# Norm sums through 64 columns, LoRA products beside the residual updates, and attention scores inside the query products

## The reference

```
h = h + 0.5 * rms_norm(swiglu(rms_norm(h, g[0]), w_in, w_out), g[1])   # pre norm, post norm
u = rms_norm(h, g[2])
# mixer: x_prev is x shifted by a token
xr, xw, xk, xv, xa, xg = [x + (x_prev - x) * mu[i] for i in range(6)]
r = xr @ w_rkv[0];  k = xk @ w_rkv[1];  v = xv @ w_rkv[2]
w = -softplus(-(w0 + tanh(xw @ w1) @ w2)) - 0.5
a = sigmoid(a0 + (xa @ a1) @ a2);  g = sigmoid(xg @ g1) @ g2
# attention: blocks of 128 queries against 256 keys, 16 query heads, 4 key heads
q = xq @ w_q + b_q
p = softmax(concat([mask(q k^T / 8), sink]))[..., :-1];  o = (p v) @ w_o + b_o
# last block
mod = c @ w_ada + b_ada
```

## Time and profile before

| | us |
|---|---|
| median of 3 runs | 2849.88 (2849.01 to 2850.76) |
| the profiled execution | 2848.1 |
| its span | 2846.2 |
| PE busy | 2700.0 (95% of the span) |
| DVE busy | 1094.9 (38%) |
| ACT busy | 627.9 (22%) |
| POOL busy | 1783.7 (63%) |
| mean granted TensorE clock | 0.966 of full |

### The profile page before, as it was taken

How to read it: one execution, slowest core, us unless ns; L and a number is a source line. 1 busy time by engine, 2 the same in 40 slices (tenths; PEclk the granted TensorE clock), 3 DMA queues, 4 the chain that set the end, 5 groups by cost and what they waited for, 6 DMA issues and landing times.

```text
span 2846.2 us, 47915 instructions
## 1 busy us (share of the span) xinstructions
PE 2700.0 (95%) x17928; PEld 2199.1 (77%) x17928; DVE 1094.9 (38%) x1624; ACT 627.9 (22%) x1203; POOL 1783.7 (63%) x1827
## 2 busy tenths in 40 slices
PE   8999988988987999999999999899999999999998
PEld 7888877767775788888888888678888888777677
DVE  3333043774554533310533303655333224123344
ACT  2111033433532211101211102343111011344211
POOL 6777768673321577776677766665777756645565
PEclk9999989989998999999999999999999989999998
DMA  4333313220000233333233332332333323322212
GB/s 138 95 95 96 96 45 88 75 57 3 4 3 12 74 89 96 95 96 94 75 96 96 96 96 78 115 133 70 97 96 96 95 72 92 90 62 67 76 42 81
DMA packets 116791, 225.94 MB, mean 79 GB/s; under 512 B 13088, under 2 KB 13856, under 8 KB 115616
## 3 DMA queue, kind: packets, MB, share of 16 engines
q1 hardware_dynamic: 114624, 209.46, 26.1%
q10 hardware_dynamic: 2016, 14.22, 1.4%
HBM read 221.53 MB, written 2.10 MB: 79 GB/s over the span
## 4 chain that ended last, share of the span: by engine, by line
PE 70%; DVE 7%; ACT 3%; issue 3%; POOL 3%; DMA 0%; DVEq 0%; POOLq 0%; ACTq 0%; SPq 0%
PE bank L222 17%; PE bank L224 17%; PE bank L223 17%; PE bank L320 1%; PE bank L1290 1%; POOL turn_a L1978 1%; DVE h L692 1%; PE bank L1305 1%; PE bank L353 1%; PE bank L2224 1%; PE bank L1240 1%; PE bank L240 1%; DVE acc L316 1%; PE bank L2215 1%; PE bank L2406 1%
## 5 line engine op out<-in xcount | busy, mean ns | idle before, releaser
L209 POOL TENSOR_TENSOR w_lo<-w_raw,w_hi 128x512 fp32r<-128x512 f32 x778 | 1045.5, 1344 | 755.5 <-PE bank L224 593.1
L222 PE MATMUL bank<-x_hi,w_hi 128*128 128x512 f32 x1904 | 751.5, 395 | 4.3 <-POOL w_lo L209 2.2
L224 PE MATMUL bank<-x_hi,w_lo 128*128 128x512 f32 x1904 | 747.8, 393 | 0.0
L223 PE MATMUL bank<-x_lo,w_hi 128*128 128x512 f32 x1904 | 742.8, 390 | 0.0
L214 POOL TENSOR_SCALAR w_hi<-w_raw 128x512 fp32r<-128x512 f32 x778 | 569.9, 733 | 4.8 <-DMA w_raw<-weights 4.8
L222 PEld LDWEIGHTS bank<-x_hi,w_hi 128*128 128x128 f32 x1904 | 358.2, 188 | 83.6 <-POOL w_lo L209 4.2
L224 PEld LDWEIGHTS bank<-x_hi,w_lo 128*128 128x128 f32 x1904 | 357.9, 188 | 80.2
L223 PEld LDWEIGHTS bank<-x_lo,w_hi 128*128 128x128 f32 x1904 | 358.1, 188 | 79.2 <-issue 0.2
L659 DVE TENSOR_TENSOR f<-bank,rstd 128x512 f32<-128x512 f32 x88 | 56.7, 686 | 595.5 <-PE bank L224 587.7
L222 PE MATMUL bank<-mid_hi,w_hi 128*128 128x512 f32 x704 | 276.4, 393 | 0.8 <-POOL w_lo L209 0.8
L224 PE MATMUL bank<-mid_hi,w_lo 128*128 128x512 f32 x704 | 276.3, 393 | 0.0
(11 more groups left out here) (426 smaller groups left out, 3584.3 us busy)
## 6 DMA issues: line engine op xcount, KB each, us to landing
w_raw<-weights SPq DMA_DIRECT2D x778, 256.0 KB, 2.6
ada_w<-ada_in ACTq DMA_DIRECT2D x8, 1536.0 KB, 6.7
h<-xT SPq DMA_DIRECT2D x4, 512.0 KB, 7.0
out<-f SPq DMA_DIRECT2D x8, 256.0 KB, 2.2
mask_b<-mask_b_in ACTq DMA_DIRECT2D x1, 640.0 KB, 5.2
spread<-spread_in SPq DMA_DIRECT2D x1, 512.0 KB, 7.5
window<-window_in ACTq DMA_DIRECT2D x1, 512.0 KB, 4.0
masks<-masks_in SPq DMA_DIRECT2D x1, 320.0 KB, 7.0
```

The source lines that it names most:

```text
L209: pool.tensor_tensor(w_lo[:, (n - 1) % RW, :], w_raw[:, (n - 1) % RS, :], w_hi[:, (n - 1) % RW, :].bitcast(F32), ALU.subtract).then_inc(w_ ...
L222: pe.matmul(outs[m], w_hi[:, s, c], hi, start=first, stop=False)
L223: pe.matmul(outs[m], w_hi[:, s, c], lo, start=False, stop=False)
L224: done = pe.matmul(outs[m], w_lo[:, s, c], hi, start=False, stop=last)
```

## The change

It has four parts.

**The mixer's head.** The updates of the first FFN move into `rwkv_vector`. ACT makes `u_hi` and DVE `u_lo` from gain times `h`, without the norm's factor, tile by tile as the updates go; PE runs the LoRA products beside them, the unshifted and the shifted half into separate banks. The factor `rstd` is applied by six DVE operations (`lora_in`) between the first x tiles. Even squares are added on DVE, odd ones on PE. POOL's six small folds become one multiplication of 128x512 with broadcast factors, and `r_gather` is made after them.

The core of the diff, its parts in the order of the text:

```
 # sums
-                done = pe.matmul(out[:, t:t + 1], src[:, t * P:(t + 1) * P], ones[:, 0:1], start=first and t == 0, ...
+                done = pe.matmul(out[:, t * 64:(t + 1) * 64], src[:, t * P:(t + 1) * P], ones[:, 0:64], start=first and t == 0, ...
+        def by_block(sums):
+            return sums[:, 0:64 * TT].rearrange("p (t c) -> p c t", c=64)[:, 0, :]
 # post norm
             unread(1)
+            norm_sums(pe, s.post, bank[s.post_at][0])
             for k in s.post.summed:
                 sum_square(pe, s.post, k, bank[s.post_at][0])
-            norm_sums(pe, s.post, bank[s.post_at][0])
         def output_scalar(act, s):
+            act.preload_act_table_set("sqrt_and_others")
...
-                if m == 3:
+                if m == 1:
                     norm_root(act, s.post, bank[s.post_at][0], D)
 # mixer, vector engine
+            for k in each:
+                update_h(dve, f0, k)
+                if k + 1 < KT:
+                    update_f(dve, f0, k + 1)
+                dve.wait_ge(*ra("u_hi", k))
+                dve.scalar_tensor_tensor(out=u_lo[:, k, 1:T + 1], in0=h[:, k, :], scalar=vcol(s.gain_in, k), in1=u_hi[:, k, 1:T + 1].bitcast(F32),
+                                         op0=ALU.mult, op1=ALU.subtract).then_inc(*rv.tell("u_lo", k))
+                add_square(dve, s.pre, k)
...
+            u_tile(0)
             dve.wait_ge(*rg("omu", 1))
             mixing(0)
+            dve.wait_ge(rstd_ready, s.rs + 1)
             for q in each:
+                if q + 1 < KT:
+                    u_tile(q + 1)
                 tile(q)
+                if 1 <= q < 7:
+                    lora_in(q - 1)
 # mixer, POOL
-                    for j, (i, a, b) in enumerate(((1, 0, 64), (4, 64, 128), (5, 128, 256)) * 2):
...
-                        pool.tensor_scalar(raw[:, c], raw[:, c], factor, None, ALU.mult).then_inc(*rg.tell("fold", k, j))
+                    columns = raw.rearrange("p (g c) -> p g c", c=64)
+                    factors_ = segments[:, k, :].unsqueeze(2).to_broadcast([P, 8, 64])
+                    pool.tensor_tensor(columns, columns, factors_, ALU.mult).then_inc(*rg.tell("fold", k))
 # attention, PE
+            for k in range(2, KT):
+                unit_products(pe, outs, x_hi[:, k, :], x_lo[:, k, :], k == 0, k == KT - 1, s.n_q + KT + k)
+                if k in (2, 4, 6):
+                    scores((2, 4, 6).index(k))
...
+                if i == STEPS:
+                    pe.wait_ge(*ad("mask", STEPS - 1))
+                for b, k in output[i - STEPS:i - STEPS + 1] if STEPS <= i < STEPS + 4 else output[4:] if i == STEPS + 4 else ():
 # attention, vector engine
-                if i in (3, 7, 11, 15):
-                    ada((3, 7, 11, 15).index(i) + 1)
+                if i < 2:
+                    ada(1, 2 * i)
+                    ada(1, 2 * i + 1)
+                elif i % 2 == 0 and 4 <= i <= 18:
+                    ada(2 + (i - 4) // 8, (i - 4) // 2 % 4)
```

More of the change, by code:

```diff
@@ L294, in square_used, with square_at @@
             eng.wait_ge(sq_summed if on_pe else sq_used, n + 1)
+        def square_at(nm, j):
+            return sq_last[:] if nm.late and j == nm.tiles - 1 else sq[:, (nm.sq0 + j) % 2, :]
         def square(act, nm, j, src, **bias):
[L297 to L300, removed]
+            g = nm.sq0 + j
+            if g >= 2 and not (nm.late and j == nm.tiles - 1):
+                square_used(act, g - 2)
+            act.activation(square_at(nm, j), src, ACT.Square, **bias).then_inc(sq_ready, 1)
         def add_square(dve, nm, j):
@@ L319, in sums_of @@
             for t in range(TT):
-                done = pe.matmul(out[:, t:t + 1], src[:, t * P:(t + 1) * P], ones[:, 0:1], start=first and t == 0, stop=last and t == TT - 1,
+                done = pe.matmul(out[:, t * 64:(t + 1) * 64], src[:, t * P:(t + 1) * P], ones[:, 0:64], start=first and t == 0, stop=last and t == TT - 1,
                                  skip_group_check=True)
@@ L340, in norm_root @@
                 act.wait_ge(sums_ready, nm.n + 1)
-            else:
+            if nm.late or not nm.added:
                 square_used(act, nm.sq0 + nm.tiles - 1)
-            act.activation(root[:], sums[:, 0:TT], ACT.Sqrt, bias=eps[:, 0:1], scale=1.0 / width).then_inc(root_ready, 1)
+            act.activation(root[:], by_block(sums), ACT.Sqrt, bias=eps[:, 0:1], scale=1.0 / width).then_inc(root_ready, 1)
         def norm_inverse(dve, nm):
@@ L803, in program @@
         PREP = "cum cm fl kk k2 b K B A0 A".split()
-        rv = Steps("rwkv_dve", ["zero", "reset", "reset0", "gn_eps"] + [("block", n) for n in range(3)] + [("u_lo", k) for k in each] + ["wa_lo", "tg_lo"] +
+        rv = Steps("rwkv_dve", ["zero", "zero_lo"] + [("u_lo", k) for k in each] + ["reset", "reset0", "gn_eps"] + [("block", n) for n in range(3)] +
+                   [(n, j) for j in range(2) for n in ("now", "back", "in")] + ["wa_lo", "tg_lo"] +
                    [(n, 0) for n in PREP[:3]] + ["max", "rec"] + [(n, 0) for n in PREP[3:]] + [(n, k) for k in (1, 2) for n in PREP] + [("R", k) for k in range(3)] + [(n, k) for k in range(3, KT) for n in PREP + ["R"]])
@@ L1460, in flat @@
             return t.rearrange("p a t -> p (a t)")
[L1462 removed]
+        SEGMENTS = (1, 4, 5, 5) * 2
+        rg = Steps("rwkv_pool", [("omu", 0), ("omu", 1)] + [("segment", j) for j in range(8)] + [("fold", k) for k in each] + [("gather", k) for k in each])
         def lora_pool(pool, s):
@@ L1791, in swa_tensor @@
             norm_beside(pe, s, outs, s.n_q + KT, KT - 1)
-            for k in range(2, KT):
-                unit_products(pe, outs, x_hi[:, k, :], x_lo[:, k, :], k == 0, k == KT - 1, s.n_q + KT + k)
             def scores(a):
@@ L1838, in values @@
                 done.then_inc(*ap.tell("value", a))
+            for k in range(2, KT):
+                unit_products(pe, outs, x_hi[:, k, :], x_lo[:, k, :], k == 0, k == KT - 1, s.n_q + KT + k)
+                if k in (2, 4, 6):
+                    scores((2, 4, 6).index(k))
+            output = [(b, k) for b in two for k in each]
             for i in ITERATIONS:
                 for a in step_at(i, 0):
-                    scores(a)
+                    if i >= 3:
+                        scores(a)
                 for a in step_at(i, 3):
@@ L1872, in swa_scalar, with biased @@
             act.activation(rstd[:], bank[s.pre_at][1][:], ACT.Copy).then_inc(rstd_ready, 1)
+            def biased(k):
+                act.wait_ge(*qv("q", k))
+                act.activation(q_t[:, k, :], q_t[:, k, :], ACT.Identity, bias=vcol("b_q", k)).then_inc(*qa.tell("bias", k))
+            for k in range(4):
+                biased(k)
+            NEXT_ADA = (1, 3, 11, 19)
             def next_ada(k):
-                act.wait_ge(*av("ada", k - 1))
-                act.dma_start(ada_w[:], ada_in[k]).then_inc(ada_loaded, 16)
+                act.wait_ge(*av("ada", k - 2, 3))
+                act.dma_start(ada_w[k % 2][:], ada_in[k]).then_inc(ada_loaded[k % 2], 16)
             for i in ITERATIONS:
```

192 lines of the change are left out of this document (107 added, 85 removed).

## The result

The changed kernel takes 2805.02 us in the median of 4 runs (2803.22 to 2807.75), against 2849.45 for the kernel before in the same comparison: a ratio of 0.9846, 95% interval 0.9829 to 0.9863. That is 44 us less where 39 were forecast; the time lies 6 us under the predicted 2811, inside the range. The profiled execution has a span of 2802.2 us against 2846.2, so the two traces show 44.0 of it.

The account below looks back on a forecast made before the run. TensorE, busy 2700.0 of 2846.2 us, was taken as the bound, leaving only stretches with gaps or low clock. Gains of 8.4, 12.4 and 18.1 sum to 38.9, from 2848.1 to 2809.2, as a median 2811 us; range 2802 to 2820.

Parts of the forecast that it names:

- the mixer's head: From the first FFN's end through the k products: end at 483.2 instead of 491.60, gain 8.4 us, bounds 2 to 15.
- The last unit and the fold: First FFN's end: POOL wait of 0.83 us goes; fold costs 1.26, its collisions with DVE 4.0 us (0 to 8).
- The root and the wide: After the FFN's sums: root 0.85 us earlier with its table preloaded, wide 1.02 us shorter if columns keep the clock up.
- The relay: Mixer's k products: first after about 5.7 us, seven further tiles 4.3 us apart, then units at 2.75 each.
- The norms' 12.4: Four other late post norms gain 0.85 and 1.0 each, 7.4 us; the inner norm 5.0; bounds 4 to 15.
- 10 us hang on the clock: Across head and norms: five wides of 1.0 us and the inner norm's 5.0 need columns to keep the clock up.
- The attention's 18.1: Attention: first turn 6.3 us earlier, thirteen steps 9.6 us shorter, tail 2.2 us shorter; bounds 9 to 25.
- The steps: Thirteen attention steps fall from 4.94 to 4.2 us each, 3.86 if PE is full; gain 9.6 us.
- The first (2821): Rival: columns don't keep the clock up, so 10 us don't come; 2821 us, chance 0.25.
- the second: Rival: DVE/ACT relay and second ada transfer halve the hoped gains, 5.2 a tile, 4.6 a step; 2823 us, chance 0.17.
- the third: Rival: 64 columns cost array time, 0.39 us a record instead of 0.13; 2903 us, chance 0.03.
- the fourth: Rival: LoRA products don't run beside updates, early scores block PE, moves only shift waits; 2849 us, chance 0.03.

Follow-up runs that it names:

- one_column: The changed kernel with one column in every norm sum instead of 64, nothing else differing; 2813.0 us, ratio 0.9879.
- columns_128: The changed kernel with 128 columns in every norm sum instead of 64; 2800.57 us, ratio 0.9844.
- before_64: The kernel before the change with 64 columns in its norm sums and the readers' stride, nothing else; 2842.11 us, ratio 0.9969.

## Why the prediction was right, and where its terms were not

The forecast was 8.4 for the mixer's head, 12.4 for the post norms and 18.1 for the attention, 38.9 in all. By the table the three gave 12.4, 6.9 and 23.3 (counting the attention's own head, 1.6, to the norms), and 1.5 came from stretches whose code is unchanged. The mechanisms were in the main the right ones; of the forms of the post norm most did not pay. That the sum came within 6 us is partly luck: two terms that were 4.0 and 5.2 too small stood against one that was 5.5 too large.

**The last unit and the fold.** That the wait of 0.83 us goes was right: PE has no wait there, and 1.0 was gained, as far as that stretch can tell. The fold was put at 1.26 us and measures 1.04, and it was charged with 4.0 us of collisions in the head. The head took 31.63 us from first update to reciprocal, 0.3 more than the FFN's 31.3: this term was the mis-sized one, and its 3.7 us are nearly all that the head gained beyond the forecast. The prediction read the price of a collision from two different operations of the earlier trace rows, 0.69 us of f times the wide and 1.62 of h plus f. In the changed kernel none of the 48 f times the wide takes more than 0.69 us. Of the 48 h plus f, 22 take 1.09 to 1.79, each started while a w_hi or w_lo of POOL was running; the others take 0.66 to 0.69, and no fold was running when any of the 48 started. Two of the head:

```profile
396.80 1.09 DVE L705 TENSOR_TENSOR h<-h,f 128x512 f32<-128x512 f32 x1
399.36 1.77 DVE L705 TENSOR_TENSOR h<-h,f 128x512 f32<-128x512 f32 x1
```

What was missed is the reverse: with six folds the overlapped products would have starved on POOL, 6.9 us. The fold in one piece is not a cost beside the overlap but most of what lets it pay.

**The root and the wide.** The wide went from 2.08 to 1.16 us as said, except behind the attention, where it still took 2.05. The root's 0.85 reached the end of a stretch clearly only in the inner norm; elsewhere summing acc first added a wait for DVE (1.59 us behind the first FFN, so the first update came at 387.51, not 386.05, and 1.48 behind the attention). The root did come right after the sums, but the sums themselves now end later. The forms together are worth 1.5 us by the medians, with no clear sign.

**The relay.** First k product 5.25 us after the first u (5.7 taken), tiles 28.34/7 = 4.05 apart (4.3), the rest 24.9 (24.75). These hold.

**The norms' 12.4.** Place by place: the fourth FFN's post and inner norm gave 6.0 (5.0 plus 1.85 forecast), the third FFN's post norm, in the attention's head, 1.6 of 1.85, the second FFN's 0.2 of 1.85. Behind the attention there were -1.8 instead of +1.85, by DVE's backlog and the low clock that followed. The mixer's post norm has the late form too; the sum had no term for it, and it gave 0.9. Behind the second FFN the first products came 1.6 us earlier after its end, but DVE's same 39 instructions took 32.31 us instead of 30.65 (h plus f alone 2.9 us more, the low parts 1.9 less), and PE then stood 2.2 us for the pre norm's reciprocal: that stretch ends with DVE, not with the wide. That 10 us hang on the clock was right in sum: 8.0 by the times, 10.2 by the trace.

**The attention's 18.1.** From the queries' last product to the first turn it was 12.4 us before (1808.25 to 1820.64) and 4.6 after (1795.47 to 1800.02): 7.8, less 3.9 by which the query products take longer (24.65 against 20.78) with three scores among them; 4.0 against 6.3. The steps gave 16.1 against 9.6: the mis-sized term. I had laid the waits on the ada pass as much as on x_lo; the runs show x_lo (16.2) and hardly the ada pass (2.5 at most), and that the step is then PE's own work, 3.70. That lies below the 3.86 that I had taken as its floor, which was read in a window with a mean clock of 0.86, where these steps had 0.97. The tail gave 3.2 against 2.2.

**The rivals.** The first (2821) fell with one_column; the second with 4.05 a tile and 3.70 a step; the third with the sums of the changed kernel, 0.13 us a record, and with columns_128; the fourth with the trace.

## What to carry to other kernels

In a program where each engine takes its work in order, look first for an instruction that waits for an engine which in turn waits for it a few places on: moving DVE's x_lo one iteration later was worth 16 of the attention's 22 us (13 in the time of the whole kernel, one run), and cutting the long pass next to it almost nothing. Work that is pushed out of a loop lands on the same engine behind it: look there for who waits, since 4.8 us of this gain went back where a sum waited for DVE and the clock fell behind the wait. When an overlap is planned, price the supply of every operand at the new rate (here POOL's folds), not only the collisions that the supplier causes.

## What was not expected of the hardware

With the granted clock up, 8 records of an fp32 sum take 1.03 us with 1 column, 1.06 with 64 and 1.06 to 1.16 with 128. Sums with 64 columns kept the clock at 1.00 where it was up in five post norms out of six; behind the attention, after PE's wait of 1.48 us, it fell with 64 columns and not with 128. And 48 records of 64 in a row didn't raise it from 0.50 once it had fallen; it rose in the LoRA products behind them.

In the profile of before_64 the third FFN takes 370.0 us where it took 361.4 before. 1.6 of the 8.6 are a clock of 0.50 from 1386.3 to 1389.7, as in the changed kernel. The rest is spread evenly over the products, with no wait of PE and the granted clock at 1.00. Here is that rest, first in the changed kernel, then in before_64 (columns as in the earlier trace rows):

```profile
1373.00:1732.60 359.60, 359.60 (x1573) 295.00 (x1572) 91.15 (x103) 32.82 (x52) 258.21 (x262) 1.00 0.33 95
1389.70:1756.30 366.60, 366.60 (x1573) 296.96 (x1573) 79.60 (x103) 31.54 (x51) 257.44 (x262) 1.00 0.33 93
```

The same 1573 records take 366.6 instead of 359.6 us, 1.9% more: 0.233 us from one product to the next instead of 0.229. The second and the fourth FFN of the same execution run at the usual pace. Something slows the products of one stage of one execution without showing in the clock; no run here tells what. The timed runs of one kernel here spread over 5 to 18 us, and this would be enough for part of it.
